# One program for several stages of a two-block transformer kernel, and tokens fetched back in two pieces

## What is computed

```python
# first block
h = modulate(rmsnorm(x, norm_mix_g), sh1, sc1)
proj = h @ w_in                                  # q, k, v, gates, merge gates
kc, vc = compress(k_cmp, ...), compress(v_cmp, ...)
o_a = g0 * o_cmp + g1 * o_sel + g2 * o_win       # three attentions
o_b = stick_breaking(q_b, k_b, v_b)
y = sigmoid(merge_0) * (o_a @ w_proj_a) + sigmoid(merge_1) * (o_b @ w_proj_b)
x = x + g1 * (y @ w_out)
x = x + g2 * swiglu(modulate(rmsnorm(x, norm_ffn_g), sh2, sc2), ...)
# second block
z = h @ w_in_2
x = x + (sigmoid(gate_a) * (y_a @ w_up_a) + sigmoid(gate_b) * (y_b @ w_up_b)) @ w_out
x = x + hier_moe(rmsnorm(x, g_ffn), ...)         # 32 experts, top 2 of one group
x = x + sigmoid(h @ w_pg) * (p @ w_ple)
```

## Time and profile before

| | us |
|---|---|
| median of 3 runs | 1868.06 |
| lowest, highest | 1867.74, 1876.9 |
| the profiled execution, its own time | 1872.86 |
| its span, first to last instruction | 1871.1 |

### The profile page before, as it was taken

One profiled execution on the slowest core, in us unless ns is written; L12 is line 12 of the kernel. 1 busy time (PEld: TensorE's weight loads), 2 busy tenths in 40 slices (PEclk: granted clock), 3 DMA queues, 4 the chain that ended last, 5 costly groups with the idle time before them and its releaser, 6 DMA issues. The chain is left out here.

```text
span 1871.1 us, 20208 instructions
## 1 busy us (share of the span) xinstructions
PE 1722.5 (92%) x8167; PEld 1179.4 (63%) x8167; DVE 803.1 (43%) x1272; ACT 529.2 (28%) x890; POOL 49.6 (3%) x89
## 2 busy tenths in 40 slices
PE   2999989989988999999989999999899989898888
PEld 2887866646677888878768876757334434343446
DVE  4763357633463222255642275234423323232345
ACT  4212246731252222232443242324100000000037
POOL 0000000100000000000000000000200000000000
PEclk9989989979998999999989999999899999999999
DMA  9764120022421332221322111218799999999961
GB/s 350 237 248 140 44 103 33 2 90 90 135 90 54 115 102 90 90 101 68 130 73 91 45 46 45 91 54 354 259 421 423 426 426 425 427 426 425 426 277 45
DMA packets 87655, 351.75 MB, mean 188 GB/s; under 512 B 9910, under 2 KB 39266, under 8 KB 71561
## 3 DMA queue, kind: packets, MB, share of 16 engines
q1 hardware_dynamic: 85002, 346.08, 47.7%
q0 software_dynamic: 2560, 4.37, 0.7%
HBM read 346.03 MB, written 8.43 MB: 189 GB/s over the span
## 5 line engine op out<-in xcount | busy, mean ns | idle before, releaser
L549 DVE TENSOR_TENSOR arena<-ring,arena 128x1024 fp32r<-128x1024 f32 x120 | 146.9, 1225 | 236.3 <-ACT arena L598 217.1
L2653 PE MATMUL ex_h<-ring,u_big_tail 128*64 128x512 f32 x512 | 154.0, 610 | 13.2 <-DMA ring<-in_w 8.3
L554 PE MATMUL up_ps<-h_high,arena 128*128 128x512 f32 x352 | 138.1, 392 | 6.9 <-PEq L180 6.2
L555 PE MATMUL up_ps<-arena 128*128 128x512 f32 x352 | 137.7, 391 | 0.0
L556 PE MATMUL up_ps<-h_high,arena 128*128 128x512 f32 x352 | 137.7, 391 | 0.0
L598 ACT CAST arena<-ring 128x1024 fp32r<-128x1024 f32 x82 | 85.9, 1047 | 161.7 <-PE up_ps L556 86.0
L2653 PE MATMUL ex_h<-s_ab,u_big_tail 128*64 128x512 f32 x272 | 114.3, 596 | 2.0 <-DVE u_big_tail L2624 1.4
L2624 DVE TENSOR_TENSOR u_big_tail<-ex_x,vcol 128x512 f32<-128x512 f32 x32 | 20.6, 686 | 179.7 <-PE ex_x L2617 179.7
L2653 PEld LDWEIGHTS ex_h<-ring,u_big_tail 128*64 128x64 f32 x512 | 47.4, 140 | 78.7 <-issue 77.6
L2919 ACT ACTIVATE u_big_tail<-ex_h 128x512 f32<-128x512 f32 x16 | 9.6, 597 | 293.8 <-PE ex_h L2653 293.8
L554 PEld LDWEIGHTS up_ps<-h_high,arena 128*128 128x128 f32 x352 | 66.6, 189 | 21.3 <-issue 6.6
(11 more groups left out here) (576 smaller groups left out, 3610.9 us busy)
## 6 DMA issues: line engine op xcount, KB each, us to landing
ring<-in_w SPq DMA_DIRECT2D x42, 2048.0 KB, 32.4
s_ab<-in_w SPq DMA_DIRECT2D x32, 2048.0 KB, 32.0
ring<-in_w_in SPq DMA_DIRECT2D x19, 2048.0 KB, 8.3
ring<-in_w_ada SPq DMA_DIRECT2D x24, 1024.0 KB, 7.0
reg_a<-in_w SPq DMA_DIRECT2D x10, 2048.0 KB, 31.5
w1flat<-in_w SPq DMA_DIRECT2D x10, 2048.0 KB
ring<-in_w_ffn_gate SPq DMA_DIRECT2D x11, 1024.0 KB, 5.4
ring<-in_w_ffn_up SPq DMA_DIRECT2D x11, 1024.0 KB, 8.0
```

Source lines behind the costliest of these rows:

```text
L549: return engine.tensor_tensor(lo, v, hi.bitcast(F32), ALU.subtract)
L554: nc.tensor.matmul(ps, x[0], y[0], start=start, stop=False)
L555: nc.tensor.matmul(ps, x[0], y[1], start=False, stop=False)
L2653: mm = nc.tensor.matmul(ps[half, :], xT[:, k, half], ws[j][:, k, cols], start=(k == 0), stop=(k == k_end - 1))
```

## The change

1. `begin_program` and `end_program` keep one `Block` open over several stages. Three programs are made: `stage_project1`, `stage_compress`, `stage_attention`, `stage_merge` and `out1`; `stage_ffn_up` and `down`; `stage_project2`, `mixed_merge` and `out2`. Seven barriers go. Those at `fresh_sems` stay, and so do those around the router.
2. What the barriers had ordered is ordered by waits on single semaphores: PSUM banks (`p1_even`, `p1_odd`, `cmp_moved_d`, `cmp_moved_a`, `cmp_kept`, `wait_banks`, `p2_ev`), work memory (`cmp_used`, `at_y`, `merge_used`) and sources of steps (`wait_source`). In `out1` and `out2` the first steps take the groups of tokens in the order 2, 3, 0, 1.
3. `gate(0)` of `stage_compress` moves to the front of PE's part, and its weights are prepared at the end of `stage_project1`.
4. `h` comes back in two pieces of 1 MB: the first without a wait for the end of attention, the second behind `at_y`. DVE no longer waits for `h` at the start of the merge, and ACT waits for each half where it casts it. The waits for `h_saved` and `x_back` move from SP to DVE.

```diff
+    def begin_program(self):
+
+        if self.block is None:
+            self.open_program = ExitStack()
+            self.block = self.open_program.enter_context(self.nc.Block())
+
+    def end_program(self):
+
+        self.open_program.close()
+        self.block = None
...
@@ stage_project1
-        block = ps_ctx.enter_context(nc.Block())
+        block = b.block
...
-            sp.wait_ge(b.h_saved, 16)
...
                 split_ahead(dve, parts.dve_w, i)
+                if tiles[i][2] == "wide" and tiles[i][1] == 0:
+                    parts.dve_w(dve, b.early0)
...
@@ stage_compress
+            gate(0)
+            pe.wait_ge(b.p1_even, 12)
+            pe.wait_ge(b.p1_odd, 11)
             for i in range(2 * KD):
                 mm = nc.tensor.matmul(ps_s[0][:, i:i + 1], b.acc2[:, D + i * P:D + i * P + P], b.ones[:, 0:1], start=True, stop=True)
...
             mm.then_inc(kcp, 1)
-            gate(0)
             pe.wait_ge(moved_rows, 2)
...
-            parts.dve_w(dve, g0)
+            dve.wait_ge(b.h_saved, 16)
...
-            parts.act_w(act, g0)
+            act.wait_ge(b.p1_even, 12)
...
@@ stage_attention
+                if i == 0:
+                    pe.wait_ge(b.cmp_moved_d, 2)
+                    pe.wait_ge(b.cmp_moved_a, 2)
...
+                if g == 0:
+                    pe.wait_ge(b.cmp_kept, 8)
...
+            pool.wait_ge(b.cmp_used, b.cmp_end)
...
@@ stage_merge
-            sp.dma_start(b.reg_a[:], b.h_dram).then_inc(b.h_back, 16)
+            sp.dma_start(b.reg_a[:, 0:4 * U], b.h_dram[:, 0:4 * U]).then_inc(h_wait, 16)
+            sp.wait_ge(b.at_y, NT)
+            sp.dma_start(b.reg_a[:, 4 * U:], b.h_dram[:, 4 * U:]).then_inc(h_back2, 16)
             sp.dma_start(b.x, x_load).then_inc(b.x_back, 16)
             b.load_until(sp, up_b + 1 + RING)
-            sp.wait_ge(b.x_back, 16)
...
+            pe.wait_ge(b.at_y, NT)
             for n in range(8):
                 project(0, n)
...
-            act.wait_ge(h_wait, 16)
+            act.wait_ge(b.at_y, NT)
             parts.act_w(act, 0)
-            parts.act_h(act)
+            for k in range(KD):
+                act.wait_ge((h_wait, h_back2)[k // 4], 16)
+                nc.scalar.copy(parts.h[0][:, k, :], b.hT[:, k, :]).then_inc(parts.h_hi, 1)
...
-            dve.wait_ge(h_wait, 16)
             parts.dve_w(dve, 0)
...
@@ stage_rows_out
+        def wait_banks(pe, t):
+
+            if kind == "mod":
+                pe.wait_ge((b.merge_prod, b.merge_sig)[t // 2], 7 + t % 2)
+            elif kind == "twice":
+                pe.wait_ge(b.up_ev, KF - 1 + t // 2)
+            elif t < 2:
+                pe.wait_ge(b.mx_used_up, 15 + t)
...
-                for t in range(NT):
+                for t in range(NT) if kind == "twice" else (2, 3, 0, 1):
+                    if k == 0:
+                        wait_banks(pe, t)
...
+                sp.wait_ge(b.mx_proj, 16)
+                sp.wait_ge(b.mx_merged, KD)
                 for m in range(4):
                     load_expert(b, sp, m)
...
@@ mixed_merge
             pe.wait_ge(b.gm_in, 48)
+            pe.wait_ge(b.p2_ev, 20)
...
             pe.wait_ge(normed, 1)
+            pe.wait_ge(b.p2_ev, 24)
...
+            dve.wait_ge(b.p2_ev, 8)
             link(nc.vector.tensor_reduce(gs[:, 0:4], gv, AX.X, ALU.add))
```

More of the change, by code:

```diff
@@ L714, in stage_project1 @@
     nc, a = b.nc, b.a
+    b.begin_program()
     b.cmp_in = b.sem("cmp_in")
@@ L873, in _ @@
                 split_ahead(act, parts.act_w, i)
+                if tiles[i][2] == "wide" and tiles[i][1] == 0:
+                    parts.act_w(act, b.early0)
                 if i % 2:
@@ L906, in stage_compress @@
         ps_pos, ps_o, F = ps_t[0], [ps_k, ps_h, *ps_s], [bank("f0"), bank("f1")]
-        block = ps_ctx.enter_context(nc.Block())
+        block = b.block
+        b.cmp_kept, b.cmp_used, b.cmp_end = kept, parts.used, g0 + 8
         @block.sync
@@ L1063, in _ @@
                 dve.wait_ge(o, n + 1)
-                nc.vector.tensor_copy(b.early_oa[:, n, :], ps_o[n][:])
+                nc.vector.tensor_copy(b.early_oa[:, n, :], ps_o[n][:]).then_inc(b.cmp_moved_d, 1)
         @block.scalar
@@ L1102, in _ @@
                 act.wait_ge(o, n + 1)
-                nc.scalar.copy(b.early_oa[:, n, :], ps_o[n][:])
+                nc.scalar.copy(b.early_oa[:, n, :], ps_o[n][:]).then_inc(b.cmp_moved_a, 1)
             keep(7)
@@ L1175, in stage_attention @@
         ps_o = [banks(f"o{i}", 1) for i in range(2)]
-        block = ps_ctx.enter_context(nc.Block())
+        block = b.block
+        b.at_y = y_made
         @block.sync
@@ L1393, in stage_merge @@
     (_, up_a), (gate_chunks, up_b) = chunks
+    h_back2 = b.sem("h_back2")
     proj, ready, sig, first, prod, ev = (b.sem(f"{name}_{n}") for n in ("proj", "ready", "sig", "first", "prod", "ev"))
@@ L1559, in stage_rows_out, with wait_source @@
         ps = [ps_ctx.enter_context(nc.psum_tensor(f"{name}_ps{i}", [P, CH], F32)) for i in range(8)]
-        block = ps_ctx.enter_context(nc.Block())
+        block = b.block
         def turn_bank(t, k):
             return ps[k // 4 * NT + t][:, k % 4 * P:k % 4 * P + P]
+        def wait_banks(pe, t):
[5 more added lines that the diff above has]
+                pe.wait_ge(b.mx_used_up, 15 + t)
+        def wait_source(act, k):
+            if kind == "mod":
+                act.wait_ge(b.merge_ev, k + 1)
+                if k == ahead:
+                    act.wait_ge(b.merge_used, 8)
+            elif kind == "twice":
+                act.wait_ge(b.up_ev, k + 1)
+                if k in (1, 2):
+                    act.wait_ge(b.up_used, 2 * KF - 2 + k)
+            else:
+                act.wait_ge(b.mx_merged, k + 1)
         @block.sync
@@ L1587, in _ @@
         def _(pool):
+            if kind == "rows":
+                pool.wait_ge(b.mx_stated, T // HG_CHUNK - 1)
             nc.gpsimd.memset(eps2, EPS * EPS).then_inc(eps_in, 1)
@@ L1679, in split @@
                                                            in1=h_hi[:, k, t * P:t * P + P].bitcast(F32), op0=ALU.mult, op1=ALU.subtract)
+            if kind == "mod":
+                dve.wait_ge(b.x_back, 16)
             add_in(0)
@@ L1702, in _ @@
             for k in range(ahead, K):
+                wait_source(act, k)
                 st.act_s(act, k)
@@ L1760, in _ @@
                 nc.scalar.activation(r1, ssx, ACT.Sqrt, scale=1.0 / D, bias=eps).then_inc(late, 1)
+    b.end_program()
     if kind == "rows":
@@ L1777, in stage_ffn_up @@
         ps = [[ps_ctx.enter_context(nc.psum_tensor(f"up_ps{i}{j}", [P, CH], F32)) for j in range(2)] for i in range(4)]
-        block = ps_ctx.enter_context(nc.Block())
+        block = b.block
+        b.up_ev, b.up_used = ev, parts.used
         @block.sync
@@ L1841, in stage_project2 @@
         ps = [ps_ctx.enter_context(nc.psum_tensor(f"p2_ps{i}", [P, CH], F32)) for i in range(8)]
-        block = ps_ctx.enter_context(nc.Block())
+        block = b.block
+        b.p2_ev = ev
         @block.sync
@@ L1940, in mixed_merge @@
         H = [ps_ctx.enter_context(nc.psum_tensor(f"mx_h{i}", [P, CH], F32)) for i in range(6)]
-        block = ps_ctx.enter_context(nc.Block())
+        block = b.block
+        b.mx_used_up, b.mx_merged, b.mx_proj, b.mx_stated = used_up, merged, proj, stated
         @block.sync
```

5 lines of the change are left out of this document (4 added, 1 removed).

## The result

| | median, us | lowest to highest | runs | mean granted clock |
|---|---|---|---|---|
| before | 1876.82 | 1867.74 to 1883.28 | 20 | 0.9695 |
| changed | 1865.75 | 1858.57 to 1870.44 | 20 | 0.9734 |

The ratio of changed to before is 0.9947, with a 95% interval of 0.9934 to 0.996: 9.9 us less, between 7.5 and 12.4. A second measurement of the same kernel, further down, gave 0.9963 (0.9947 to 0.9978). (The mean clock of before is that of 29 other executions, taken beside a later experiment; its three such sets gave 0.9695 to 0.9707.) The profiled execution took 1866.27 us, with a span of 1863.9; before's had 1872.86 and 1871.1.

The account below looks back on a forecast made before the run. PE, nearly always busy, was taken as the bound, with seven barrier waits of 15.3 us; +3.5 - 2.3 - 4.5 - 7.1 = -10.4 us gave 1857.7 us from the median (1862.5 for the profiled execution), range 1850 to 1866.

Parts of the forecast that it names:

- the chances of 0.57 and 0.37: Whole kernel: 0.57 for faster and 0.37 for same, with 0.5% (9.3 us) as the bound between them.
- Project1 to compress: Project1's end to compression's products: a loss of +3.5 us from `win` losing its cover; bounds +1.6 to +5.4.
- 3.7 + 2.3 + 1.9: Compression ahead of L954: column sums 3.7 us, row sums with positions 2.3, the other half of the row sums 1.9.
- one stretch, 1.9: Behind the wait for `win`: one stretch of PE at the lower clock, costing 1.9 us, a price taken from the merge.
- Compress to attention: Start of attention: -2.3 us, as PE scores at once but ACT's sigmoid holds the gain between 1.5 and 2.9.
- Attention to merge: Start of merge: -4.5 us, the 2.4 us bank wait and the lower-clock stretch of 1.9 behind it go, plus 0.2.
- the case of the bound, -2.6: Merge: the gain is only 2.6 us if the clock falls all the same.
- The other four: Merge to `out1` and mixed to `out2` -3.0 together, up to down -1.7, project2 to mixed -2.4: -7.1 us.
- The carry to the end: Behind the router: PE and the expert weight stream both start earlier, so the whole gain reaches the kernel's end.
- The gain shrinks: Rival, chance 0.30: `win` +5.4, attention -1.5, merge -2.6, the rest -7.1; in all -5.8 us, 1862.3.
- The clock holds: Rival, chance 0.12: no lower clock at `win`; -12.3 us, 1855.8.
- the branches: Rival, chance 0.06: branches between stages in merged programs fetch their targets and stall engines; at 6 us a fetch, 1882.5.

Follow-up runs that it names:

- the halves: Two kernels: changed with barriers back ahead of `down`, mixed and `out2`, 0.9995 of before; before with only those three barriers taken out, 0.9983.
- the kernel with `gate(0)` late: The changed kernel with PE's `gate(0)` back behind the turned positions; 1859.25 us, 0.992 of before.
- project1 and compress alone: Before with only project1 and compress in one program, `gate(0)` first, all other barriers kept, `h` in one piece; 1883.88 us, 1.0041 of before.

## Why the prediction was right and wrong

**The level.** The forecast took its difference from a median of three runs, which stood at the low end of what before does (1867.74 to 1883.28). It named the 8.8 us by which a run lay above that median, but put only 3.7 on top of its worst sum in the range, and none in the forecast; 1865.75 is inside 1850 to 1866 by a quarter of a microsecond, which is luck. From the median of twenty, 1876.82 - 10.4 = 1866.4, and 1865.75 was measured. From the profiled execution it said 1862.5; that of the changed kernel took 1866.27.

**The difference.** 11.1 us between the medians, 9.9 by the ratio, 6.9 in the second measurement (0.9963), 6.6 between the profiled executions. The 10.4 is near the first, but not for its reasons: two errors cancel in part. The compression term was too small, and the sum without compression was -13.9 and is -17.0 in the traces, of which 2.0 are the lower clock at attention's end and 0.7 the part behind the router, which the forecast had no reason to expect. That is luck. The clock has a part in the times too: at the 1.3 us per 0.001 given below, 0.9734 against 0.9695 to 0.9707 is an estimated 3.5 to 5.1 of the 9.9 us. Why the changed kernel is granted more clock over the whole, with less of it in compression, is not shown. As to the bound of 0.5%, the first ratio is just beyond it and the second inside: the chances of 0.57 and 0.37 were not badly placed.

**Project1 to compress: the term mis-sized.** This is the step that failed. The mechanism was right: the cover is lost, the wait is 4.5 us (4.6 forecast), and the clock falls behind it. The size was not: +9.8 in this pair of traces, +7.7 (4.3 to 11.3) by time, against +3.5. Of the excess in the traces, 3.1 us are the step "3.7 + 2.3 + 1.9", which let the sums run at full speed because a dense `gate(0)` now stood ahead of them: they took 10.96 instead of 7.9 (9.3 in some executions, so 1.4 to 3.1). The other 3.5 are "one stretch, 1.9": first products and `gate(1)` lost 5.4. The price of 1.9 had been taken from one stretch in the merge and was carried to another wait. Most of what was measured lies above the upper bound of two stretches, +5.4. The new start of L954 was given as 202.1 and is 204.8.

**Compress to attention: right.** -2.3 forecast; PE gained 3.0, the scan 2.5. ACT did bound it, as said, with a new PE wait of 1.6 us. POOL's `dist` and the six biases, which DVE forms, were not in the way: the biases are over at 277.01, and POOL's mask ends at 277.44.

**Attention to merge: the wait right, the clock not, and the wrong part credited in the change.** The wait of 2.4 for the bank is gone. -4.5 was forecast, of which 1.9 was a stretch at the lower clock that should go with it. The merge gained 3.0, since its first products still ran at the lower clock; the case of the bound, -2.6, came true. Whether they do is not set by the wait: behind the same wait of 2.9 us for L1322 the first gate came 28.0 us behind the first projection in one execution, 29.7 in four (the forecast's "29") and 31.0 in six. The forecast named the second half of `h` as not critical; it did not say that the first is not either.

**The other four: right.** Merge to `out1` -1.4 (-1.5). Up to down -2.2 (-1.7), project2 to mixed -2.0 (-2.4), mixed to `out2` -2.5 (-1.5): 6.7 in the pair against 5.6, and 5 to 7.5 by the halves. The carry to the end held in this pair: 0.7 of 6.5 us changed behind the router. It can't be tested finely, as that part took 559.2 to 564.6 us over the 14 profiled executions. The first expert weight was issued at 1304.41 instead of 1310.93, 6.5 earlier and not 10 to 13, which only repeats the miss in compression.

**The rivals.** "The gain shrinks" had the right place, and two of its three terms came true: `win` at its +5.4 or more, and the clock falling in the merge; attention gained more than its -1.5. Its -5.8 is nearer to the second measurement, 6.9, than the forecast is. "The clock holds" was wrong: it fell twice. No run shows a cost of the branches. At `out1`, where PE's branch stands behind the wait for its own product, the gap is 0.33 us, as at `merge_g`, which has no branch. At the merge PE's wait for `at_y` stands behind the branch, so that its 2.9 us would cover a fetch. The Trainium skill (Runtime: NRT & Kernel Launch, Instruction fetch mechanics) says that a taken branch out of the pages held stalls the engine. If the target at `out1` lay outside them, a fetch should have shown there, and this trace has no room for one; where the target lay no run shows.

## What to carry to other kernels

When a barrier is removed, look first at what ran under it or under the work moved ahead of it: here 5.6 us of cover moved away cost as much as all the barriers of the first program gave. Order PE's cheap, sparse work so that it covers the other engines' preparation, and keep it mixed with dense products; that brought as much again as the change. And before a difference of half a per cent is turned into a time, know the level of before from more than three runs, and what stages with the same code do from more than two traces.

## What the runs showed of the hardware

**Idle time and the clock.** In six profiled executions PE stood 2.1 or 4.5 us ahead of the first compression products, and in all six these took 6.8 to 7.1 us. In eight, before's among them, it stood there for 0.95 us or less, and in all eight they took 3.7 to 3.8. The Trainium skill (TensorE: Matmul & The Clock Gate, HAM oscillation) describes this for kernels whose PE waits on transfers: the next work starts slow. The trace agrees at this place, for a wait on DVE.

But the length of the wait does not settle it. Ahead of the merge's first projection PE stood for 2.9 to 3.2 us in all 14 executions, and in 12 the clock fell behind it. In the kernel with `gate(0)` late and in that with project1 and compress alone it did not; the granted clock stayed at 1.00:

```profile
394.90 27.73 PE L543 MATMUL merge_p<-s_ab,ring 128*128 128x512 f32 x64 [2.88 <-DVE s_ab L1322]
404.67 7.11 PE L548 MATMUL merge_p<-s_ab,ring 128*128 128x512 f32 x16 [3.15 <-PEq L176]
```

The changed kernel took 30.68 for the same 64 products, and before 8.80 for the same 16. What decides between the two is open.

**One-column products and the clock.** Sixteen column sums in a block (3.6 to 4.6 us, 6.4 in one trace, PE busy throughout) were followed in all twelve profiled executions that had them by a first row sum of 1.7 to 2.1 us instead of 1.0, straight behind `gate(0)` too. Spread over `gate(1)` they were not. A busy PE is not always a PE that keeps its clock.

The 64 products of 32 columns that form compression's scores are a second case. They take 8.4 to 11.0 us, with no wait of PE among them. In all 14 executions the granted clock was 1.00 as they began and fell 3 to 6 us later, and PE ran at 1.2 GHz for the next 7 to 14 us. No run changed them, so the narrow columns as the cause are argued by the likeness to the column sums, and not shown.

**The spread of the runs.** The clock accounts for most of it. The changed kernel's runs at a mean granted clock of 0.975 to 0.977 took 1858.6 to 1862.6 us, those at 0.970 to 0.973 took 1865.4 to 1870.4. Over all runs of this study, with a level of its own for each kernel, 0.001 of granted clock went with 1.3 us.
